# A hybrid pooling and attention decoder layer on one core: the first stage's loads and transposes in another order

## The reference, cut to what matters

```python
def decoder_layer(x, c, start_pos, attend, pool_buf, lam_init, alpha, w_ada, b_ada, w_in, ...):
    mod = (silu(c) @ w_ada + b_ada)[:, None, :]            # c: 1 + 8 rows of 1024; w_ada 1024 x 6144
    sh1, sc1, g1, sh2, sc2, g2 = split(mod, 6, axis=-1)
    h = x * (1 + sc1) + sh1                                # x: 1024 + 8 rows of 1024
    proj = h @ w_in                                        # w_in: 1024 x 5632
    q, k, v, u, gates = split(proj, ...)
    q = rope(q, pos); k = rope(k, pos)                     # the rotary table
    lam = exp(sum(lambda_q1 * lambda_k1)) - exp(sum(lambda_q2 * lambda_k2)) + lam_init
    attn_out = head_rmsnorm(attend(q, k, v, lam), subln_g) * (1 - lam_init)
    pool_out = pool_mixer(pool_buf, u, ...) * pool_scale   # windowed means of u, a map per group
    merged = sigmoid(g_pool) * pool_out + sigmoid(g_attn) * attn_out
    x = layer_norm(alpha * x + (1 + g1) * (merged @ w_out))
    h2 = x * (1 + sc2) + sh2
    return layer_norm(alpha * x + (1 + g2) * hier_moe(h2)), k, v, new_pool
```

## Time and profile before

| | us |
|---|---|
| Median of 3 runs (lowest to highest) | 1399.42 (1398.91 to 1400.55) |
| The profiled execution, its own time | 1400.47 |
| Its span, first to last instruction | 1398.6 |
| PE busy in it | 1284.5 (92%) |
| DVE busy | 999.7 (71%) |
| ACT busy | 742.3 (53%) |
| POOL busy | 129.6 (9%) |
| The first stage ends (first instruction of the second) | 61.80 |

### The profile page before, as it was taken

How to read it: one execution, slowest core, us unless ns; L and a number is a source line. 1 busy time by engine, 2 the same in 40 slices (tenths; PEclk the granted TensorE clock), 3 DMA queues, 4 the chain that set the end, 5 groups by cost and what they waited for, 6 DMA issues and landing times.

```text
span 1398.6 us, 25507 instructions
## 1 busy us (share of the span) xinstructions
PE 1284.5 (92%) x9230; PEld 1111.2 (79%) x9230; DVE 999.7 (71%) x1528; ACT 742.3 (53%) x1322; POOL 129.6 (9%) x95
## 2 busy tenths in 40 slices
PE   4699999999999999999999997999389999999966
PEld 3588999999999999999999974877278887888832
DVE  2533457577585875858758667599779998999948
ACT  1444334454455454554544555422338988999835
POOL 1533200000000000000000000000011111111042
PEclk9899999999999999999999998999669999999988
DMA  9887343223332333322333343463177989555866
GB/s 319 259 266 242 123 126 101 72 84 94 92 116 57 94 97 93 114 60 86 104 94 108 89 131 103 146 213 136 75 268 259 373 290 376 205 186 184 282 250 198
DMA packets 210982, 229.47 MB, mean 164 GB/s; under 512 B 17942, under 2 KB 184794, under 8 KB 210747
## 3 DMA queue, kind: packets, MB, share of 16 engines
q1 hardware_dynamic: 195627, 173.39, 39.7%
q0 software_dynamic: 6976, 25.23, 5.4%
q10 hardware_dynamic: 8280, 29.51, 5.3%
HBM read 173.07 MB, written 46.79 MB: 157 GB/s over the span
## 4 chain that ended last, share of the span: by engine, by line
PE 71%; DVE 10%; DMA 7%; ACT 5%; issue 3%; SPq 3%; POOL 2%; ACTq 0%; DVEq 0%; POOLq 0%
PE AB L991 11%; PE AB L995 11%; PE AB L992 11%; PE S L916 5%; PE S L918 5%; PE S L917 5%; PE S L1089 4%; ACT F L1494 3%; PE T L1115 3%; DMA F<-in_w_e_up 2%; DMA F<-in_b_ada 2%; ACT R L1494 2%; PE OB L916 2%; PE OB L918 1%; PE OB L917 1%
## 5 line engine op out<-in xcount | busy, mean ns | idle before, releaser
L1494 ACT ACTIVATE R<-F 128x1024 fp32r<-128x1024 f32 (+4 forms) x305 | 292.3, 1006 | 76.6 <-DVE F L2073 39.4
L991 PE MATMUL AB<-R 128*128 128x344 f32 x960 | 315.1, 332 | 1.2 <-ACT F L1494 1.2
L992 PE MATMUL AB<-R 128*128 128x344 f32 x960 | 303.8, 320 | 0.0
L916 PE MATMUL S<-R 128*128 128x512 f32 x480 | 192.2, 400 | 1.9 <-ACT F L1494 1.6
L918 PE MATMUL S<-R 128*128 128x512 f32 x480 | 187.9, 391 | 0.0
L917 PE MATMUL S<-R 128*128 128x512 f32 x480 | 187.6, 391 | 0.0
L991 PEld LDWEIGHTS AB<-R 128*128 128x128 f32 x960 | 181.2, 189 | 4.8 <-issue 4.7
L992 PEld LDWEIGHTS AB<-R 128*128 128x128 f32 x960 | 181.5, 189 | 1.7 <-issue 1.7
L995 PE MATMUL AB<-R 128*128 128x344 f32 x960 | 171.6, 320 | 0.0
L1494 ACT ACTIVATE F<-AB 128x344 f32<-128x344 f32 (+3 forms) x129 | 59.1, 460 | 209.6 <-PE AB L995 195.6
L995 PEld LDWEIGHTS AB<-R 128*128 128x128 f32 x960 | 155.6, 188 | 0.0
(11 more groups left out here) (292 smaller groups left out, 2261.7 us busy)
## 6 DMA issues: line engine op xcount, KB each, us to landing
F<-in_w_ada SPq DMA_DIRECT2D x24, 1024.0 KB
F<-in_w_in SPq DMA_DIRECT2D x44, 512.0 KB, 4.1
F<-in_w_e_gate SPq DMA_DIRECT2D x16, 1024.0 KB, 5.8
F<-in_w_e_up SPq DMA_DIRECT2D x16, 1024.0 KB, 10.8
F<-in_w_e_down SPq DMA_DIRECT2D x16, 1024.0 KB, 11.1
y_d<-F ACTq DMA_DIRECT2D x32, 512.0 KB, 7.6
out<-F SPq DMA_DIRECT2D x24, 512.0 KB, 4.1
F<-F SPq DMA_DIRECT2D x192, 43.0 KB, 1.9
```

Source lines behind the costliest of these rows:

```text
L916: mm(out, w[0], m[1], start=start, stop=False)
L991: mm(bank[:, 0:PIECE], whl[b][0][:, k, :], x[1][:, k, :], start=(k == 0), stop=False)
L992: mm(bank[:, 0:PIECE], whl[b][0][:, k, :], x[0][:, k, :], start=False, stop=False)
L1494: return nc.scalar.activation(out, in_, func, **kw)
```

## The change

On SP, the input rows are loaded between modulation chunks 0 and 1 instead of after 1; the seven small loads come after chunk 4 and ahead of chunks 5, 6 and 7; the rotary table is loaded in the second stage, behind chunk 15. On PE and DVE, the first two modulation chunks are turned and copied first, and then two h pieces follow each chunk (one block of features), where before four followed every second chunk. On DVE the lambda operations move from behind chunk 7 to behind chunk 6, and the sample rows' operations ahead of the last two pieces. On ACT the high part of the first `w_in` chunk is made before the exponential of lambda, and on POOL its low part is made at the start of the second stage. DVE's first rotary operation now waits for the table.

```diff
             ada(0)
-            ada(1)
             for t in range(NT):
                 sp.dma_start(xr[:, t, :], x_p[t * P:(t + 1) * P, :]).then_inc(ld_x, 16)
                 if t == 3:
-                    ada(2)
+                    ada(1)
             sp.dma_start(xr[0:NS, NT, :], x_s).then_inc(ld_x, 16)
-            for n in range(3, EARLY):
+            for n in range(2, 5):
                 ada(n)
-            sp.dma_start(cossin, I["rope"]).then_inc(ld_small, 16)
             sp.dma_start(sublng, ...)      # and pscale, pt, four lambda rows: unchanged
+            for n in range(5, EARLY):
+                ada(n)
...
-            sp.wait_ge(ld_small, 16 * 8)
+            sp.wait_ge(ld_small, 16 * 7)
...
             for n in range(EARLY + 5, NADA):
                 ada(n)
                 if n == EARLY + 7:
+                    sp.dma_start(cossin, I["rope"]).then_inc(state_st, 16)
                     sp.dma_start(O[7][0, :, 0:BUF - 1, :], I["state_pool"][0, :, 1:BUF, :]).then_inc(state_st, 16)
```

PE:

```diff
-        for n in range(EARLY):
+        ada(0, Sb[0])
+        ada(1, Sb[1])
+        modulation(0)
+        modulation(1)
+        x_columns(0)
+        pe.wait_ge(modT_copied, 2)
+        for k in range(KC):
+            last = tr(OB[:, 64 + NS * k:64 + NS * k + NS], xr[0:NS, NT, k * P:(k + 1) * P], ident[0:NS, 0:NS])
+        last.then_inc(cT_done, 1)
+        for n in range(2, EARLY):
             if n >= 4:
                 pe.wait_ge(ada_row, n - 3)
             ada(n, Sb[n % 4])
-            if n >= 1:
-                modulation(n - 1)
-            if n >= 2 and n % 2 == 0:
-                x_columns(n // 2 - 1)
...
-        modulation(EARLY - 1)
-        x_columns(EARLY // 2 - 1)
+            if n % 2 == 0:
+                x_columns(n - 1)
+                modulation(n)
+            else:
+                modulation(n)
+                x_columns(n - 1)
+        x_columns(EARLY - 1)
```

DVE, ACT and POOL:

```diff
-        for n in range(EARLY):
+        ada_sum(0, Sb[0])
+        ada_sum(1, Sb[1])
+        mod_columns(0)
+        mod_columns(1)
+        h_part(0)
+        h_part(1)
+        for n in range(2, EARLY):
             ada_sum(n, Sb[n % 4])
-            if n >= 1:
-                mod_columns(n - 1)
-            if n >= 2 and n % 2 == 0:
-                for m in range(2 * n - 4, 2 * n):
-                    h_part(m)
-        dve.wait_ge(ld_small, 16 * 8)
-        ...                                # lambda: two products and a sum
-        mod_columns(EARLY - 1)
+            if n % 2:
+                mod_columns(n)
+            for m in (2 * n - 2, 2 * n - 1):
+                h_part(m)
+            if n % 2 == 0:
+                mod_columns(n)
+            if n == 6:
+                dve.wait_ge(ld_small, 16 * 7)
+                ...                        # lambda: the same three
         dve.wait_ge(cT_done, 2)
         V(TT(hs32, OB[:, 64:128]..., modT[:, 8:16, 1:9], ALU.mult))
-        for m in range(12, 16):
-            h_part(m)
         mark(TT(hs32, hs32, modT[:, 0:8, 1:9], ALU.add), hs_ready, 1)
+        h_part(14)
+        h_part(15)
...
             if m == 11:
+                w_split(0)
                 act.wait_ge(lam_sum, 1)
                 act_(lamt[:, 0:2], lamt[:, 2:4], ACT.Exp).then_inc(lam_exp, 1)
-                w_split(0)
...
-            if m == 11:
-                w_rest(0)
         pool.wait_ge(h_lo, 16)
         stage_end(pool, 0)
...
+        w_rest(0)
         late(EARLY)
```

More of the change, by code:

```diff
@@ L449, in _build @@
     tab_landed = sem("tab_landed")
-    m_landed = [Again(sem(f"m_landed{i}"), 0) for i in range(2)] + [Again(state_st, 16)]
+    m_landed = [Again(sem(f"m_landed{i}"), 0) for i in range(2)] + [Again(state_st, 32)]
     m_hi, m_lo = sem("m_hi"), sem("m_lo")
@@ L535, in _build @@
     g2b, l2g, l2b = [f.take(D) for _ in range(3)]
-    x5_landed = [Again(ld_c, 48), Again(ld_x, 16 * 9), Again(ld_small, 16 * 8)]
+    x5_landed = [Again(ld_c, 48), Again(ld_x, 16 * 9), Again(ld_small, 16 * 7)]
     y5_landed = [Again(s_, 16 * (SLOT_TILES // 2)) for s_ in xg_landed] + [Again(sem(f"y5_landed{i}"), 0) for i in range(2, NT + 1)]
@@ L943, in modulation, with x_columns @@
             last.then_inc(modT_done, 1)
-        def x_columns(q):
-            for m in range(4 * q, 4 * q + 4):
+        def x_columns(p):
+            for m in (2 * p, 2 * p + 1):
                 if m == 0:
@@ L952, in x_columns @@
                 for t in range(4):
-                    last = tr(TB[m % 2][:, t * P:(t + 1) * P], xr[:, 4 * (m % 2) + t, (m // 2) * P:(m // 2 + 1) * P], ident)
+                    last = tr(TB[m % 2][:, t * P:(t + 1) * P], xr[:, 4 * (m % 2) + t, p * P:(p + 1) * P], ident)
                 last.then_inc(xT_done, 1)
-        for n in range(EARLY):
+        ada(0, Sb[0])
[8 more added lines that the diff above has]
+        for n in range(2, EARLY):
             if n >= 4:
@@ L2086, in mod_columns @@
                  modT_copied, n + 1)
-        for n in range(EARLY):
-            ada_sum(n, Sb[n % 4])
-            if n >= 1:
-                mod_columns(n - 1)
-            if n >= 2 and n % 2 == 0:
-                for m in range(2 * n - 4, 2 * n):
-                    h_part(m)
-        dve.wait_ge(ld_small, 16 * 8)
-        V(TT(lamv[:, 0, :], lamv[:, 0, :], lamv[:, 1, :], ALU.mult))
-        V(TT(lamv[:, 1, :], lamv[:, 2, :], lamv[:, 3, :], ALU.mult))
-        mark(rsum(lamt[:, 2:4], lamv[:, 0:2, :]), lam_sum, 1)
-        mod_columns(EARLY - 1)
+        ada_sum(0, Sb[0])
[5 more added lines that the diff above has]
+        for n in range(2, EARLY):
+            ada_sum(n, Sb[n % 4])
+            if n % 2:
[6 more added lines that the diff above has]
+                dve.wait_ge(ld_small, 16 * 7)
+                V(TT(lamv[:, 0, :], lamv[:, 0, :], lamv[:, 1, :], ALU.mult))
+                V(TT(lamv[:, 1, :], lamv[:, 2, :], lamv[:, 3, :], ALU.mult))
+                mark(rsum(lamt[:, 2:4], lamv[:, 0:2, :]), lam_sum, 1)
         dve.wait_ge(cT_done, 2)
         V(TT(hs32, OB[:, 64:128].rearrange("p (k b) -> p k b", k=8), modT[:, 8:16, 1:9], ALU.mult))
-        for m in range(12, 16):
-            h_part(m)
         mark(TT(hs32, hs32, modT[:, 0:8, 1:9], ALU.add), hs_ready, 1)
+        h_part(14)
+        h_part(15)
         dve.wait_ge(lam_exp, 1)
@@ L2148, in rope @@
             turn = 6 * h + n
+            if turn == 0:
+                dve.wait_ge(state_st, 32)
             cols = slice((n % 3) * PIECE, (n % 3 + 1) * PIECE)
```

## The result

The changed kernel takes 1402.93 us (median of 20 runs, 1399.58 to 1405.89); the kernel before, beside it on the same chips, 1399.16 (20 runs, 1396.45 to 1405.04). The ratio is 1.0026, with a 95% interval of 1.0017 to 1.0034: slower, by 3.8 us in the medians, where 3.1 less was forecast.

A forecast was written before the change was run, and what follows sets the result against it. The prediction took two chains ending together to bound the first stage, the loads (60.1) and DVE's (61.7). It summed -4.3 (stage) + 1.2 (clock) + 0 (second stage) = -3.1, giving 1396.3 us against 1399.42; range 1393.4 to 1399.6.

The forecast's parts named there:

- the thing to see: First stage, SP's queue at 44 to 48 before the change: something in the small loads blocks it some 4.5 us.
- first step: First stage: chunk 5, behind the small loads' hole, lands at 39.8; a late issue could make it 41.5.
- bound of 40.2: Upper end for chunk 5's landing in the first stage: 30.0 + 10.2, from the earlier w_in chunk's 8.7 plus 1.5.
- rival 2: First stage: longer hole, small loads issued later against the queue's end; chunk 5 at 41.5, time 1398.6; chance 0.15.
- second step: First stage, from chunk 5's landing to the end: 17.6 of work plus 1.2 for the fallen clock, ending at 58.7.
- third step: Second stage: the moved low part and rotary table cost 0, at most 1 each.
- the queue has work meanwhile: Second stage's start: half a megabyte of w_in and another of pooling weights ahead of chunk 11; cost 0, at most 1.
- loads' chain: First stage: chunks 6, 7, w_in, 8 and 9 behind chunk 5 take 14.2, so chunk 9 lands at 54.0.
- rival 3: Second stage gives the gain back, chunk 11 or 16 late; waits together at most 2, time 1398.3; chance 0.07.
- rival 4: First stage: the clock does not come back after the quiet stretch; time 1400.9 to 1401.6; chance 0.08.

The follow-up runs named there:

- e4: Kernel before with only the rotary table's load moved behind chunk 15 in the second stage; ratio 0.9998 to the kernel before.
- e2: Changed kernel with POOL's low part of the first w_in chunk back between h pieces 11 and 12; ratio 1.0025 to the kernel before.
- a1: Changed kernel with SP loading chunk 11 ahead of the third w_in chunk and chunk 12 ahead of the fourth; ratio 1.0007 to the kernel before.
- k1: Changed kernel with 24 throwaway transpositions on PE ahead of its wait for chunk 11; ratio 1.0022 to the kernel before.
- h0: Kernel before with only the seven small loads moved ahead of chunk 5; ratio 1.0033 to the kernel before.
- e1: Changed kernel with the seven small loads back behind chunk 7, ahead of the first w_in chunk; ratio 0.9998 to the kernel before.
- e5: Changed kernel with the seven small loads issued by ACT on its own queue, behind its first operation; ratio 1.0003 to the kernel before.
- c1: Changed kernel with all seven small loads issued by ACT between h pieces, lambda's operations moved to the second stage; ratio 1.0009 to the kernel before.
- d1: Changed kernel with lambda's rows behind chunk 7 and POOL's low part back between pieces 11 and 12; ratio 0.9989 to the kernel before.
- g1: Changed kernel with only lambda's four row loads moved behind chunk 7; ratio 0.9986 to the kernel before.
- c2: c1 with POOL's low part of the first w_in chunk back between pieces 11 and 12; ratio 1.0006 to the kernel before.
- g2: Changed kernel with pool_scale, subln_g and the page table behind chunk 7, lambda's rows staying ahead of chunk 5; ratio 1.0001 to the kernel before.

## Why the prediction was wrong

**Right.** The rows came earlier, by 1.96 where 3.15 was forecast (23.1 forecast, 24.29 measured). A hole opened in the windows (0.28 over 30 to 38), ahead of chunk 5, and the clock fell while PE waited (at about 39.4; 41.6 was forecast). It fell again after PE's wait for chunk 7's sum and during the one for chunk 11. The Trainium skill ("TensorE: Matmul & The Clock Gate", section "HAM oscillation — how this bites in real kernels") says that waits on loads between bursts of matmuls bring the clock down; the falls at 39.4 and at chunk 11 agree with it. The table's move costs nothing that can be measured (e4). The prediction even named the thing to see: small loads that block the queue.

**Wrong, first step: when chunk 5 lands.** I took 39.8, with 41.5 as the price of a late issue. The changed kernel has 42.44; the other kernels with all seven loads ahead of chunk 5 have 39.98 (e2), 42.08 (a1), 42.28 (k1) and 42.52 (h0). So the bound of 40.2, worked out from the half-size `w_in` chunk of the earlier trace rows, was near the lower end of what happens. This term is 2.6 short. What failed in it, by the traces, is the point that it counts from. The bound took the 8.7 from the end of the transfers, at 30.0; in the kernel before, the issue of the load behind the hole (43.30) falls together with that end, so the two could not be told apart. In the changed kernel SP issued chunk 5 only at 32.67, and it reached PE 9.8 after its issue, as in a1, k1 and h0 (9.8 each, issued at 32.3 to 32.7); e2 issued it at 31.25 and had it 8.7 later. That is the mechanism of rival 2, which had 0.15 and was priced at 41.5.

**Wrong, second step: from chunk 5 to the stage's end.** I had 17.6 and 1.2 for the clock, 18.8; measured are 21.7 (42.44 to 64.14). The half clock lasted some 10 us, in place of a few, and chunk 5 itself ran in it: piece 10 starts 8.2 after chunk 5, where the sum had 6.0, so the fall cost up to 2.2, 1.0 more than I had. Lambda's three operations took 2.1 (0.82, 1.02 and 0.28) where I counted 0.8: 1.3 more, on the path. In their new place POOL works on two h pieces beside them (52.17 to 54.31). Alone such a product takes 0.23, and so it does in e1, in the same place of DVE's list, where POOL stood idle from 46.5 to 54.0:

```profile
49.12 0.23 DVE L2112 TENSOR_TENSOR F<-F 128x64 f32<-128x64 f32 x1 [4.21 <-DMA F<-in_lambda_k]
49.38 0.23 DVE L2113 TENSOR_TENSOR F<-F 128x64 f32<-128x64 f32 x1
```

The small operations at the end took 2.8 (61.37 to 64.17), not 2.2.

**Wrong, third step: the second stage.** I gave it 0, at most 1. It lost 4 more in the traces. That a1 takes back 0.19% by an edit of the second stage alone points the same way in the medians. The reasoning failed in one sentence, "the queue has work meanwhile": at 63 to 65 and 65 to 68 the share is 0.17 and 0.66. SP's queue starts empty at the boundary and then waits for the low part (done at 66.57) before it issues the third `w_in` chunk (66.64), with chunk 11 behind it (68.76). The low part's place, though, is not the whole of that: with it back (e2) the trace gains but the median does not. What takes the loss back is another order of SP's loads (a1, d2). And about 1 us of the 13.6 belongs to this one execution: in the eleven other edited kernels with the old order of SP's loads in the second stage, chunk 11 came 11.8 to 12.7 after the start, and in k1, with the same loads as here, 12.6.

**What the sum missed as a whole.** I treated the hole as a cost that only moves. h0 says what the move is worth: from behind chunk 7, where the kernel before has it, to ahead of chunk 5 it costs 0.33%. What it costs behind chunk 7 no run shows: e1 equals the kernel before, but both have it there, and PE idles beside it (6.76 in e1); e5 and c1, which took the small loads out of SP's queue, were no faster, but each changed something else as well. Ahead of chunk 5 all the modulation chunks still to come stand behind it, and the late sums then keep chunks 8 and 9 out of their buffers, which opens two further holes (48 to 52, 55 to 57). My loads' chain ("chunk 9 lands at 54.0") left that wait for buffers out; chunk 9 started on PE at 62.42.

The forecast's chances failed with it: rival 3 (the second stage gives it back) had 0.07 and was priced at 2 at most, and rival 4's clock had to do alone what three terms did together. In sum 2.6 + 2.9 + 4 turn -3.1 into +6.4 by POOL's mark in the traces; the medians say +3.8. In the pair of traces 3.0 of the 6.4 goes again behind 830, beside a slightly higher granted clock; the late chunk 11 of this one execution is another part. Beyond that, why the traces show more at POOL's mark than the medians do at the end is not settled. Nor is why chunk 5 lands at 40 in some executions and at 42 in others with the same queue.

## What to carry to other kernels

A small load is dear by its place in the queue, not by its bytes: do not put loads of many short runs ahead of a load that an engine waits for, and move a block of them only after asking who stands behind it (h0: 0.33% for the move alone). When forecasting the landing of a load behind such a block, count from its own issue, not from the end of the transfers before. A gain before a stage boundary is kept only if the first load wanted beyond it comes earlier too; where an engine waits for a load there, reorder the loads in the same change (d1's edits and the new order of loads together gave 0.3%, the latter alone nothing measurable). And where a load waits for a buffer, carry the lateness of the engine that frees it into the loads' own chain.

## What the runs showed of the hardware that was not expected

- Four loads of 32 KB, one row copied to 128 partitions each, keep a queue's share at 0.30 for 3 us (g1) that at other times moves 303 GB/s; with the pooling scale, the page table and the sub-normalisation's table ahead of them it is 0.14 for 7 us (h0). Issued from ACT's queue between 4 and 11 us all seven left the share at 0.93 to 1.12 there, but the rows came at 25.63 in place of 22.09 to 24.29 (e5).
- A DVE product of 128x64 takes 0.23 while POOL idles (e1) and 0.82 or 1.02 in the changed kernel, while POOL works. The operation on 128x1 columns at 61.37 takes 0.76 beside POOL, and the one at 62.16, with a single tensor as its input, 0.15 beside it.
- After a wait of 3.0 or more for chunk 11 (changed, e1, g1, c1, c2, d1) chunk 11 ran in 1.89 or 1.90; after 1.90 or less (before, e2, e4, e5, h0, a1) in 1.08. g2, with 3.55, took 1.43. The loss by it could not be measured (k1).
